# First layer of a two-block network: three modulation tiles leave the v stage and are loaded and summed in the output stage

## The reference, cut to what matters

```python
sh1, sc1, g1, sh2, sc2, g2 = jnp.split(silu(c) @ ada_w[0] + ada_b[0], 6, axis=-1)   # six modulation rows of 1024
h = rmsnorm(x, norm_mix_g[0]) * (1 + sc1) + sh1
y = mlstm_mixer(h, ...)      # qk columns, v, o (output gate), then hh @ w_out
x = x + g1 * y
h = rmsnorm(x, norm_ffn_g[0]) * (1 + sc2) + sh2      # input of the peer (expert) stage
```

## Time and profile before

| what | before |
|---|---|
| median of three runs | 2551.74 us |
| the profiled execution's own time | 2551.07 us |
| its span from first to last instruction | 2549.2 us |
| TensorE busy | 2505.4 us, 98% of the span |
| VectorE busy | 2037.1 us, 80% |
| ScalarE busy | 1421.3 us, 56% |
| GpSimd busy | 319.1 us, 13% |
| moved by DMA | 492.37 MB, mean 193 GB/s |

### The profile page before, as it was taken

The page is one execution under the profiler, slowest core; times in us unless marked ns, Lnnn a source line. Parts: engine busy times, 40 slices in busy tenths (PEclk is TensorE's granted clock), DMA queues, the critical chain, the costliest instruction groups (busy, mean ns, idle before and its releaser), DMA issues.

```text
span 2549.2 us, 45952 instructions
## 1 busy us (share of the span) xinstructions
PE 2505.4 (98%) x16116; PEld 2242.2 (88%) x16116; DVE 2037.1 (80%) x3621; ACT 1421.3 (56%) x2305; POOL 319.1 (13%) x181
## 2 busy tenths in 40 slices
PE   7999999999999999999999999999999999999998
PEld 6789989999888888889999999888888888889887
DVE  7789878899888878679888998666667886688766
ACT  4455575545566666655675545666564555463553
POOL 4017600000000004537400000000000001000000
PEclk8999999999999999999999999999999999999999
DMA  7845565445888875435665445555555355553654
GB/s 269 289 165 166 197 233 167 158 158 175 290 301 293 288 265 151 134 127 171 213 198 180 158 159 181 193 195 198 195 192 189 117 188 183 191 173 109 197 182 140
DMA packets 138421, 492.37 MB, mean 193 GB/s; under 512 B 18704, under 2 KB 18792, under 8 KB 137984
## 3 DMA queue, kind: packets, MB, share of 16 engines
q1 hardware_dynamic: 135600, 481.90, 57.0%
q0 software_dynamic: 2640, 8.02, 1.0%
HBM read 488.79 MB, written 1.07 MB: 192 GB/s over the span
## 4 chain that ended last, share of the span: by engine, by line
PE 89%; DVE 6%; DMA 2%; ACT 2%; issue 1%; POOL 1%; SPq 0%; DVEq 0%; ACTq 0%; POOLq 0%
PE ps L241 71%; PE ps L247 7%; PE ps L248 4%; PE ps L1512 2%; DMA weight_ring<-in_stream 1%; DVE weight_split L276 1%; ACT weight_split L267 1%; POOL weight_split L276 1%; PE ps L2682 1%; PE ps L1476 1%; DVE hT_split L501 1%; DVE stat L626 0%; DVE x L623 0%; PE ps L455 0%; DVE hT_split L500 0%
## 5 line engine op out<-in xcount | busy, mean ns | idle before, releaser
L267 ACT ACTIVATE weight_split<-weight_ring 128x1024 fp32r<-128x1024 f32 x800 | 849.2, 1063 | 210.2 <-DMA weight_ring<-in_stream 121.8
L276 DVE TENSOR_TENSOR weight_split<-weight_ring,weight_split 128x1024 fp32r<-128x1024 f32 x685 | 831.2, 1222 | 147.1 <-ACT weight_split L267 144.1
L241 PE MATMUL ps<-hT_split,weight_split 128*128 128x256 f32 x7224 | 918.6, 285 | 3.6 <-POOL weight_split L276 1.0
L241 PE MATMUL ps<-weight_split,hidden_split 128*128 128x512 f32 x3948 | 911.3, 390 | 0.0
L241 PEld LDWEIGHTS ps<-hT_split,weight_split 128*128 128x128 f32 x7224 | 880.0, 191 | 11.0 <-issue 6.2
L241 PEld LDWEIGHTS ps<-weight_split,hidden_split 128*128 128x128 f32 x3948 | 736.1, 188 | 156.1 <-issue 1.0
L276 POOL TENSOR_TENSOR weight_split<-weight_ring,weight_split 128x1024 fp32r<-128x1024 f32 x115 | 280.1, 2442 | 114.8 <-ACT weight_split L267 84.4
L247 PE MATMUL ps<-hT_split,weight_split 128*128 128x512 f32 x816 | 291.4, 398 | 0.5 <-DVE hT_split L501 0.5
L1607 ACT ACTIVATE hidden_split<-arena 128x256 fp32r<-128x256 f32 (+1 forms) x256 | 175.0, 684 | 184.3 <-PE ps L241 183.5
L1781 DVE TENSOR_TENSOR hidden_split<-arena,hidden_split 128x256 fp32r<-128x256 f32 x256 | 164.0, 640 | 94.9 <-ACT hidden_split L1607 94.8
L248 PE MATMUL ps<-hT_split,weight_split 128*128 128x256 f32 x816 | 229.0, 281 | 0.0
(11 more groups left out here) (376 smaller groups left out, 1915.1 us busy)
## 6 DMA issues: line engine op xcount, KB each, us to landing
weight_ring<-in_stream SPq DMA_DIRECT2D x912, 512.0 KB, 3.6
arena<-gate_rows SPq DMA_DIRECT2D x3, 512.0 KB, 4.8
x<-in_x SPq DMA_DIRECT2D x1, 1024.0 KB, 5.0
arena<-mlstm_m_rows POOLq DMA_DIRECT2D x1, 1024.0 KB, 6.3
arena<-in_ln_mix_g POOLq DMA_DIRECT2D x2, 512.0 KB, 5.9
arena<-in_ln_mix_b POOLq DMA_DIRECT2D x2, 512.0 KB, 7.8
arena<-in_ln_ffn_g POOLq DMA_DIRECT2D x2, 512.0 KB, 4.2
arena<-in_ln_ffn_b POOLq DMA_DIRECT2D x2, 512.0 KB, 6.5
```

Of the source, the lines that this page charges most:

```text
L241: mm = pe.matmul(out_, stationary(s_part), moving(m_part), start=start and n == 0, stop=stop and n == 2, skip_group_check=True)
L267: act.activation(wsplit[:, n % SPLITS, HIGH, :], ring[:, slot(POS[n]), :], ACT.Copy).then_inc(high_ready, 1)
L276: eng.tensor_tensor(w[:, REST, :], ring[:, slot(POS[n]), :], w[:, HIGH, :].bitcast(fp32), ALU.subtract).then_inc(split_ready, 1)
```

## The change

The v stage keeps an "a" tile behind v0 to v4 only; v5, v6 and v7 follow one another. The "a" tiles of the o stage are now numbers 21 to 35 instead of 24 to 38. The output stage gets an "a" tile behind each of out0, out1, out2 and out3 (36 to 39) instead of one behind out4. The whole number of tiles is the same. VectorE's sums follow: three fewer in the v stage, and in the output stage one before `two_out(2)`, one behind `variance(1)`, one behind `rstd(1)`, and the last, 39, where it was. In the place of tile 38, behind gated(6), stands tile 35.

```diff
-SEGMENTS = [("ada", "a", 16), ("mlstm", "s", 8), ("mlstm_v", "sa", 8), ("mlstm_o", "saa", 7), ("mlstm_o_end", "sa", 1),
-            ("mlstm_out", "s", 4), ("mlstm_out_ada", "sa", 1), ("mlstm_out_end", "s", 3),
+SEGMENTS = [("ada", "a", 16), ("mlstm", "s", 8), ("mlstm_v", "sa", 5), ("mlstm_v_end", "s", 3), ("mlstm_o", "saa", 7), ("mlstm_o_end", "sa", 1),
+            ("mlstm_out", "sa", 4), ("mlstm_out_end", "s", 4),
...
             for c in range(3, 8):
                 rest(dve, ML_T + 8 + c)
-                ada_dve(16 + c, ml_acc[:, 1])
+                if c < 5:
+                    ada_dve(16 + c, ml_acc[:, 1])
             weigh(0)
             rest(dve, ML_T + 16)
-            for a in (24, 25):
+            for a in (21, 22):
                 ada_dve(a, ml_acc[:, 1])
             rest(dve, ML_T + 17)
             for h in range(8):
                 if h < 6:
-                    for a in (26 + 2 * h, 27 + 2 * h):
+                    for a in (23 + 2 * h, 24 + 2 * h):
                         ada_dve(a, ml_acc[:, 1])
...
                 if h == 6:
                     gated(6)
-                    ada_dve(38, ml_acc[:, 1])
+                    ada_dve(35, ml_acc[:, 1])
                     rest(dve, ML_O)
                     two_out(0)
...
+            ada_dve(36, ml_acc[:, 1])
             two_out(2)
             rest(dve, ML_O + 2)
             variance(1)
+            ada_dve(37, ml_acc[:, 1])
             rest(dve, ML_O + 3)
             rstd(1)
+            ada_dve(38, ml_acc[:, 1])
             rest(dve, ML_O + 4)
             two_out(4)
             ada_dve(39, ml_acc[:, 1])
```

## The result

The changed kernel took **2557.75 us** (median of 13 runs, 2556.12 to 2559.15), the kernel before 2551.74 us (13 runs, 2550.16 to 2554.47). The ratio is 1.0023 with a 95% interval of 1.0015 to 1.0031: 6.0 us slower, where 5.6 us were forecast.

A forecast was written before the change was run, and what follows sets the result against it. TensorE, busy 98% of the span, was taken as the bound. Output-stage waits, with the 0.2 us gain counted in, gave +5.6: 2551.07 + 5.6 = 2556.7, plus 0.67 to the median, 2557.3 us; range 2551.5 to 2560.5.

The forecast's parts named there:

- the walk through the output stage: Output stage, followed from freed slots through late loads to TensorE's waits: end at 173.5 instead of 167.9, +5.6 us.
- The step that set the end: Output stage: sum 39 frees out7's slot late, out7's rest ends at 167.3, then 27 matmuls take 6.2 us.
- The landing of 3.2 us: Output stage: a load alone lands 3.2 us after issue; every 0.33 us more or less moves the result by 1.0.
- The gain of 0.2 us: v stage: only the 0.21 us wait before o0 can go, taken as 0.2 us and carried through the o stage.
- VectorE's time alone, 1.45 us: Output stage, every load in time: three added sums, 3.4 us, less a 1.75 us pause and 0.2 us of room.
- v3, v4 and v5 wait as before: v stage sign: these waits, 4.39 us together, lie in the unchanged part, so nothing of them goes.
- the granted clock is 1.00 throughout: Sign for the changed profile: TensorE's clock never falls to its lower level, despite expected pauses of 2.0, 3.1 and 0.7 us.
- the waits of v3 to v5 shrink: v stage: a sign that would show the prediction wrong; no size of shrinking was given.
- The clock rival: Output stage: lower clock from the second pause on, 27 matmuls take 12.4 us; +11.8 in all, 2563.5 us, chance 0.07.
- the +6.2 that I gave: End of the output stage: added time if the 27 remaining matmuls ran at the lower clock, 12.4 instead of 6.2 us.

The follow-up runs named there:

- the short sums: The changed kernel with sums 36, 37 and 38 over 128 of the 1024 columns: 2556.85 us, ratio 1.0018, +4.4 us against the kernel before.

## Why the prediction was right, and where its steps were not

**The direction and the size** came from the walk through the output stage, and the runs bear its cause out from four sides: VectorE's time without late loads costs 2.0 us, late loads with little of VectorE's time 4.4, the same work with slots freed earlier 1.3, and with the clock held through out3 the wait for out6 grows and the time stays. Each of these costs has a share of the clock in it: some 1.4 us of the 2.0, and in the profile of the short sums 1.6 of the 4.4.

**That the number came so near is partly luck.** For the profiled execution 5.6 us were forecast and 5.4 measured: the stage cost 6.9 us where the walk had 5.8, and out0 started 1.5 us earlier where the prediction had 0.2. The two misses point opposite ways and nearly cancel. The clock's cost, which the forecast put at nothing, is within the 6.0 us of the median.

**The step that set the end was right in its form.** Forecast and measured, for the first profile: sum 36 ends at 142.3 and 141.2; out3 is issued at 142.8 and 142.0, lands at 147.6 and 146.4; the reciprocal ends at 152.0 and 150.9; sum 39 ends at 159.6 and 158.9; out7 is issued at 159.7 and 159.0, and its rest is done at 167.3 and 166.9. These are times from the start of the span, and I took the stage to begin at 141.6 where it began at 140.3. Counted from there, out3 lands after 6.0 us in the walk and 6.1 in the trace, the reciprocal ends after 10.4 and 10.6, sum 39 after 18.0 and 18.6, and out7's rest after 25.7 and 26.6.

**Mis-sized terms, which partly cancel:**
- The landing of 3.2 us. out7's took 3.7, issued at 159.0 with two more loads behind it (159.6 and 160.2), and out5's 3.7 too. The row of a nearly lone load was not the nearest one for the first of a burst. The walk also had out5's high run without a wait: in the trace it waits 0.96 us for its load, and sum 39, which frees out7's slot, stands behind it. Out5's wait and out7's landing, 1.5 us together, are more than the 0.9 us that out7's rest comes late; out4's load came 0.4 us earlier than in the walk.
- The gain of 0.2 us. Out0 started 1.49 us earlier in the first profile: 0.23 before v3, 0.53 from v3 to v6, 0.37 from v6 to o0, 0.36 in the o stage. The last two are the change's, 0.7 us. I had counted only the wait that the profile shows before o0 and not what the o stage loses without a listed wait. The first two lie in tiles that the change doesn't move. Over all twelve profiles the step from v3 to v6 follows the landing of v5's load, counted from its issue: 10.78 us with 4.80 in this profile, 11.31 with 5.27 before. Profiles of the changed stream alone reach from 10.39 us (4.39) to 11.54 (5.50), so 0.53 us lies inside the scatter of loads. Whether the change has a share in it isn't shown.
- VectorE's time alone, 1.45 us, measured 2.0. I placed the wait at out7; it is at the spread of heads 4 to 7 (0.56 us), and most of the cost is the clock behind it.

**Two signs that failed.** The prediction listed "v3, v4 and v5 wait as before" and "the granted clock is 1.00 throughout", and it called itself wrong if the waits of v3 to v5 shrink. They shrank: v4 and v5 had waited 1.77 us together and now don't wait. The sign was badly chosen. In nine of the twelve profiles the clock fell behind the pause before v3, and the longer v3 fills v4's wait; how long v5's wait is depends on its load.

**The clock rival.** I gave it 0.07, with a fall behind the second pause, since the 2.62 us pause before v3 had shown no loss. One profile was too little for that. v0 to v5 have the same places in every kernel, and behind the pause of 2.5 to 2.9 us before v3 the clock fell in nine profiles and stayed up in two, the two with the stream of before (in the twelfth it had fallen behind a pause before v2). Whether the later tiles have a hand in that isn't shown. The pause of the earlier trace rows, 8.8 to 9.2 us in all twelve, was followed by 0.50 in five of them and by 1.00 in seven. So the length of a pause alone doesn't say whether the clock falls.

In the output stage the clock fell behind the first pause in all six profiles with three added sums in the stage and nothing put into the pause, and behind the second in four of the five profiles that have that pause. Its price was not the +6.2 that I gave: ahead of out6 it is hidden in the wait for loads, behind out6 it was 0 in the first profile and 1.6 to 2.8 us in the others. The Trainium skill, "TensorE: Matmul & The Clock Gate", section "HAM oscillation — how this bites in real kernels", tells of a kernel in which waits for DMA of some 3 to 5 us between bursts of matmuls let the clock fall, so that each burst starts at the lower level. The profiles show the same here behind shorter pauses, of 0.56 to 3.63 us, and a pause of 2.62 us without a fall. How much of the 6.0 us is the clock's stays open within these 0 to 2.8 us, since the profiles differ among themselves.

## What to carry to other kernels

When tiles are moved in a ring that is refilled in order, ask what frees the slot of each later tile and when: a cheap consumer placed late in its engine's list makes a load late, and the loads behind it too. Before a stage with idle DMA takes more tiles, walk one landing time from each freeing instruction to the first use. And when an added load is wanted, put its consumer where the tile is there already, not where the engine seems to have room: here the same four sums one place earlier were worth 4.6 us.

## What was not expected of the hardware

A pause of TensorE of only 0.56 us was followed by the lower clock level in three kernels (out3 4.31 to 4.44 us for 3.03), while one of 0.22 us was not. A pause of about 2.6 us before v3 was not followed by it in the kernel before, and one of some 9 us near the start was followed by it in only five of twelve profiles.

With sixteen back-to-back transposes in the pause the clock fell, and with fourteen matmuls of 256 columns in the same place it did not. That the kind of work makes the difference isn't shown: 0.71 us of pause were left behind the transposes and 0.17 behind the matmuls, and pauses of 0.56 us were followed by a fall where one of 0.22 was not.

The first of a burst of three 512 KB loads, out7's with two more within 1.2 us behind it, landed after 3.35 to 3.74 us in six profiles; in the kernel before out3's and out7's landed after 3.1 and 3.3.
